# Two units moved in the queue of the second block's heads, and a weight sum made by a transfer that adds

## What is computed

```python
def _mla_block(qn, qr, qpos, kn, kr, v, kpos):
    logits = (jnp.einsum('bqhd,bkhd->bhqk', qn, kn, ...)
              + jnp.einsum('bqhr,bkr->bhqk', qr, kr, ...)) * MLA_SCALE
    mask = (kpos // CHUNK)[None, :] <= (qpos // CHUNK)[:, None]
    p = jax.nn.softmax(jnp.where(mask, logits, NEG_INF), axis=-1)
    return jnp.einsum('bhqk,bkhd->bqhd', p.astype(v.dtype), v)
...
    o = o.reshape(B, T, MLA_WIDTH) * jax.nn.silu(gate)
    return x + o @ w_out
```

## Time and profile before

| | us |
|---|---|
| median of 3 runs (2145.31 to 2145.38) | 2145.35 |
| the profiled execution: device time | 2145.84 |
| its span, first to last instruction | 2144.1 |
| TensorE busy | 2133.9 |
| VectorE busy | 1213.3 |
| ScalarE busy | 995.8 |
| GpSimd busy | 249.7 |

### The profile page before, as it was taken

How to read it: one execution, slowest core, us unless ns; L and a number is a source line. 1 busy time by engine, 2 the same in 40 slices (tenths; PEclk the granted TensorE clock), 3 DMA queues, 4 the chain that set the end, 5 groups by cost and what they waited for, 6 DMA issues and landing times.

```text
span 2144.1 us, 33654 instructions
## 1 busy us (share of the span) xinstructions
PE 2133.9 (100%) x11609; PEld 1870.8 (87%) x11609; DVE 1213.3 (57%) x2781; ACT 995.8 (46%) x2287; POOL 249.7 (12%) x261
## 2 busy tenths in 40 slices
PE   9999999999999999999999999999999999999999
PEld 7888888888888888888888988888899999998899
DVE  6555554545555555556223344443467777777986
ACT  5544444434444444453223433443366666665433
POOL 1000000000000000000000001421332001021011
PEclk9999999999999999999999999999999999999999
DMA  5333333333233333333442333343332212122451
GB/s 185 107 104 114 105 104 89 114 109 98 94 105 104 104 110 108 104 101 115 146 136 80 112 100 94 122 137 122 127 102 83 57 50 64 50 67 90 153 172 63
DMA packets 127462, 225.30 MB, mean 105 GB/s; under 512 B 21104, under 2 KB 75120, under 8 KB 127264
## 3 DMA queue, kind: packets, MB, share of 16 engines
q1 hardware_dynamic: 127392, 224.36, 33.4%
HBM read 191.42 MB, written 32.89 MB: 105 GB/s over the span
## 4 chain that ended last, share of the span: by engine, by line
PE 94%; DVE 3%; ACT 1%; issue 1%; DMA 1%; POOL 0%; SPq 0%; ACTq 0%; DVEq 0%; POOLq 0%
PE bank L214 67%; PE bank L2653 8%; PE bank L2004 4%; PE bank L961 1%; PE bank L937 1%; PE bank L2709 1%; PE bank L2687 1%; PE bank L2703 1%; PE bank L953 1%; PE bank L1997 1%; PE bank L2689 1%; PE bank L929 1%; PE bank L2681 1%; PE bank L271 0%; DVE h_tlo L1882 0%
## 5 line engine op out<-in xcount | busy, mean ns | idle before, releaser
L214 PE MATMUL bank<-b_whi,x_hi 128*128 128x512 f32 x1016 | 401.4, 395 | 0.2
L214 PE MATMUL bank<-b_whi,x_lo 128*128 128x512 f32 x1016 | 396.5, 390 | 0.0
L214 PE MATMUL bank<-b_wlo,x_hi 128*128 128x512 f32 x1016 | 396.5, 390 | 0.0
L197 DVE SCALAR_TENSOR_TENSOR b_wlo<-b_raw,first,b_whi 128x512 fp32r<-128x512 f32 x254 | 179.4, 747 | 140.8 <-ACT b_whi L184 139.8
L184 ACT ACTIVATE b_whi<-b_raw,first 128x512 fp32r<-128x512 f32 x254 | 169.4, 715 | 160.2 <-PE bank L214 133.1
L214 PEld LDWEIGHTS bank<-b_whi,x_lo 128*128 128x128 f32 x1016 | 190.7, 188 | 40.8
L214 PEld LDWEIGHTS bank<-b_whi,x_hi 128*128 128x128 f32 x1016 | 191.0, 188 | 36.6 <-DVE b_wlo L197 0.8
L214 PEld LDWEIGHTS bank<-b_wlo,x_hi 128*128 128x128 f32 x1016 | 191.0, 188 | 35.3
L214 PE MATMUL bank<-m_whi,x_hi 128*128 128x512 f32 x320 | 125.0, 391 | 0.0
L214 PE MATMUL bank<-m_wlo,x_hi 128*128 128x512 f32 x320 | 124.6, 389 | 0.0
L214 PE MATMUL bank<-m_whi,x_lo 128*128 128x512 f32 x320 | 124.6, 389 | 0.0
(11 more groups left out here) (547 smaller groups left out, 5362.9 us busy)
## 6 DMA issues: line engine op xcount, KB each, us to landing
b_raw<-w_fox SPq DMA_DIRECT2D x127, 512.0 KB, 3.5
m_raw<-w_mla SPq DMA_DIRECT2D x40, 512.0 KB, 3.5
c_raw<-w_out SPq DMA_DIRECT2D x32, 512.0 KB, 3.5
h_ring<-w_out2s SPq DMA_DIRECT2D x16, 768.0 KB, 6.0
f_raw<-w_ukv SPq DMA_DIRECT2D x16, 512.0 KB, 3.6
queries<-e_q SPq DMA_DIRECT2D x16, 480.0 KB, 4.5
e_raw<-w_uq SPq DMA_DIRECT2D x32, 192.0 KB, 2.5
f_qa<-queries SPq DMA_DIRECT2D x16, 320.0 KB, 3.7
```

The costliest lines, as they stand in the source:

```text
L197: op = eng.scalar_tensor_tensor(lo[:, k, :], raw[:, k, :], self.gain[:, K:K + 1], hi32[:, k, :], ALU.mult, ALU.subtract)
L214: op = eng.matmul(out, a, w[:, k, :], start=(first and k == 0 and i == 0), stop=(last and k == self.kk - 1 and i == len(pairs) - 1))
```

## The change

In `MlaHead.ORDER` T6 now stands between p2 and p1 (it stood behind p1), and T7 between p0 and g (it stood behind g). In `Fast` the signs are arranged so that each sum of weights is an addition into the first block; the sum that VectorE formed behind P6 (for P7) is now made by a transfer that GpSimd issues (`grow`), which loads a block from memory a second time and adds it to the one in the ring when P3's splits no longer need it. So VectorE forms three sums per round instead of four. The roles, ring slots and the sequence of loads follow from it; SP may issue the load of role 3 once the first sum is formed. Where a result has the other sign, an addition becomes a subtraction, and two of the four sums of activations use `scalar_tensor_tensor`.

```diff
-    ROLE = {"P1": 0, "P5": 0, "P6": 0, "P3": 2, "P7": 1, "P2": 2, "P4": 0}
-    FORMED = {"P5": 0, "P6": 1, "P7": 2, "P4": 3}
-    FORM_AFTER = {"P1": 0, "P5": 1, "P6": 2, "P2": 3}
+    ROLE = {"P1": 0, "P5": 0, "P6": 0, "P4": 0, "P3": 1, "P7": 1, "P2": 3}
+    LOADED = (0, 2, 1, 3)
+    FORMED = {"P5": 0, "P6": 1, "P4": 2}
+    FORM_AFTER = {"P1": (0, 2), "P5": (1, 1), "P2": (2, 3)}
+    SLOT = ((0, 1, 2, 2), (1, 0, 2, 2))
...
             for h in range(2):
-                self.formed.wait(sp, r, 8 + 2 * h + 2)
-                self.wait_split(sp, r, "P3", 2 * h + 1)
+                self.formed.wait(sp, r, 2 * h + 2)
                 self.load(sp, r, 3, h)
...
-                    self.formed.wait(sp, r, 12 + 2 * h + 2)
-                    self.wait_split(sp, r, "P2", 2 * h + 1)
-                    self.load(sp, r + 1, 1, h)
+                    self.formed.wait(sp, r, 8 + 2 * h + 2)
+                    self.load(sp, r + 1, 2, h)
...
-                    self.load(sp, r + 1, 2, h)
+                    self.load(sp, r + 1, 1, h)
...
-    def form(self, pool, r, j, u):
-        k = slice(2 * u, 2 * u + 2)
-        a, b, c = (self.ring[self.slot(r, i)][:, k, :] for i in range(3))
-        p, dst, x, y, role = (("P1", a, b, a, 1), ("P5", a, c, a, 2), (None, b, c, b, None), ("P6", a, c, a, 3))[j]
...
+    def grow(self, pool, r):
+        x = self.ring[self.slot(r, 1)]
+        for h in range(2):
+            self.wait_split(pool, r, "P3", 2 * h + 1)
+            pool.dma_start(x[:, 4 * h:4 * h + 4, :], self.w[r, 1, h], accum_op=ALU.add).then_inc(self.grown[h].sem, 16)
+
+    def form(self, dve, r, p, u):
+        i, role = self.FORM_AFTER[p]
+        k = slice(2 * u, 2 * u + 2)
+        x = self.ring[self.slot(r, 0)][:, k, :]
+        self.wait_split(dve, r, p, u)
+        self.arrived(dve, r, role, u)
+        dve.tensor_tensor(x, x, self.ring[self.slot(r, role)][:, k, :], ALU.add).then_inc(self.formed.sem, 1)
...
     def pool(self, pool):
         for r in range(self.ROUNDS):
+            self.grow(pool, r)
             self.join(pool, r, "P6")
             self.join(pool, r, "P7")
...
+        elif p == "P7":
+            self.grown[u // 2].wait(act_, r, 1)
...
     ORDER = ["kp", "T0", "T1", "s3", "ka", "T2", "s2", "new", "T3", "s1", "s0", "T8", "sa", "sb", "T4",
-             "p3", "T5", "pn", "p2", "p1", "T6", "on", "p0", "g", "T7", "ont", "qr", "qn", "o"]
+             "p3", "T5", "pn", "p2", "T6", "p1", "on", "p0", "T7", "g", "ont", "qr", "qn", "o"]
...
-        for role in range(3):
+        for role in (0, 2, 1):
             for half in range(2):
                 fast.load(sp, 0, role, half)
```

More of the change, by code:

```diff
@@ L1694, in __init__ @@
         self.in_ = [[s(f"h_in{i}{h}", 1, 16) for h in range(2)] for i in range(3)]
-        self.t_hi, self.t_lo, self.formed = s("h_t_hi", 4 * n), s("h_t_lo", 4 * n), s("h_formed", 16)
+        self.t_hi, self.t_lo = s("h_t_hi", 4 * n), s("h_t_lo", 4 * n)
+        self.grown, self.formed = [s(f"h_grown{h}", 1, 16) for h in range(2)], s("h_formed", 12)
         self.used, self.done = s("h_used", 3 * n), s("h_done", 2 * n)
@@ L1706, in slot @@
     def slot(self, r, role):
-        return (r + role) % 3
+        return self.SLOT[r][role]
     def view(self, x, k, q):
@@ L1727, in arrived @@
     def arrived(self, eng, r, role, u):
-        n = {0: 0, 1: 1, 2: 2, 3: 2}[role]
-        i = self.slot(r, n)
-        loads = [(q, role_) for q in range(self.ROUNDS) for role_ in range(4) if self.slot(q, min(role_, 2)) == i]
+        i = self.slot(r, role)
+        loads = [(q, x) for q in range(self.ROUNDS) for x in range(4) if self.slot(q, x) == i]
         self.in_[i][u // 2].wait(eng, 0, loads.index((r, role)) + 1)
     def load(self, sp, r, role, h):
-        i = self.slot(r, min(role, 2))
-        sp.dma_start(self.ring[i][:, 4 * h:4 * h + 4, :], self.w[r, role, h]).then_inc(self.in_[i][h].sem, 16)
+        i = self.slot(r, role)
+        sp.dma_start(self.ring[i][:, 4 * h:4 * h + 4, :], self.w[r, self.LOADED[role], h]).then_inc(self.in_[i][h].sem, 16)
     PIECES = [(0, 0), (1, 1), (0, 1), (1, 0)]
@@ L1827, in join @@
             x = self.R[:, 2 * a:2 * a + 2, n * self.N:(n + 1) * self.N]
-            pool.tensor_tensor(x, x, self.both[:], ALU.add).then_inc(self.joined.sem, 1)
+            pool.tensor_tensor(x, x, self.both[:], ALU.subtract if n else ALU.add).then_inc(self.joined.sem, 1)
     def pool(self, pool):
         for r in range(self.ROUNDS):
+            self.grow(pool, r)
             self.join(pool, r, "P6")
@@ L1838, in add_up @@
         a11, a12, a21, a22 = (self.view(self.o, k, q)[:, part, :] for q in range(2) for k in range(2))
-        dst, x, y, op = ((a22, a21, a22, ALU.add), (a21, a11, a21, ALU.subtract), (a11, a22, a11, ALU.subtract),
-                         (a12, a12, a11, ALU.subtract))[i]
+        n = (0 if part.start == 0 else 4) + i
         if i:
-            self.summed.wait(dve, 0, (0 if part.start == 0 else 4) + i)
-        dve.tensor_tensor(dst, x, y, op).then_inc(self.summed.sem, 1)
+            self.summed.wait(dve, 0, n)
+        if i < 2:
+            op = dve.tensor_tensor(*((a22, a22, a21, ALU.subtract) if i == 0 else (a21, a11, a21, ALU.subtract)))
+        else:
+            x, y = (a11, a22) if i == 2 else (a12, a11)
+            op = dve.scalar_tensor_tensor(x, y if i == 2 else x, -1.0, x if i == 2 else y, ALU.mult, ALU.subtract)
+        op.then_inc(self.summed.sem, 1)
     SPLIT_SUMS = ["P5", "P6", "P3", "P7"]
@@ L1874, in hi @@
             self.formed.wait(act_, r, 4 * self.FORMED[p] + u + 1)
+        elif p == "P7":
+            self.grown[u // 2].wait(act_, r, 1)
         elif u % 2 == 0:
-            self.arrived(act_, r, 3 if p == "P2" else self.ROLE[p], u)
+            self.arrived(act_, r, self.ROLE[p], u)
         self.before(act_, r, p, u)
@@ L1929, in take @@
                 y = self.both[:, m, :] if p == "P1" else self.bank(r, p, m)[:, 0:self.N]
-                dve.tensor_tensor(x, x, y, ALU.add).then_inc(self.taken.sem, 1)
+                dve.tensor_tensor(x, x, y, ALU.subtract if at and at[1] else ALU.add).then_inc(self.taken.sem, 1)
         if p in self.NEWS:
@@ L1939, in take @@
                 x = self.R[0:NEW, SM, n * self.N:(n + 1) * self.N]
-                dve.tensor_tensor(x, x, self.tmp[:], ALU.add).then_inc(self.new_added.sem, 1)
+                dve.tensor_tensor(x, x, self.tmp[:], ALU.subtract if p == "P1" and n else ALU.add).then_inc(self.new_added.sem, 1)
     def dve(self, dve, early):
@@ L1948, in dve @@
                     if p in self.FORM_AFTER:
-                        self.form(dve, r, self.FORM_AFTER[p], u)
+                        self.form(dve, r, p, u)
                     if r == 0 and u == 3 and j < len(self.SPLIT_SUMS):
```

## The result

The changed kernel takes 2153.85 us (median of 6 runs, 2152.85 to 2154.57) against 2145.40 for the kernel before: a ratio of 1.0037, 95% interval 1.0027 to 1.0047; the medians lie 8.4 us apart. The forecast was 2152.1. The profiled execution has a span of 2151.1 us.

A forecast was written before the change was run, and what follows sets the result against it. TensorE, busy 2133.9 of 2144.1 us, was taken as the bound, so only its waits could yield gains. From 2145.35, +9.5 in the heads and -2.8 in `Fast` gave 2152.1 us, range 2149.5 to 2158.0.

The forecast's parts named there:

- p1's wait covered, -0.23: Heads: T6 ahead of p1 covers p1's wait for VectorE's low half of p3, saving 0.23 us per head.
- g's copy behind g, +0.83 per head: Heads: without T7 behind g, qr waits for ScalarE's copy of g; 1.38 us against 0.55 of work.
- A head of 23.77: Steady loop: one head lengthens by 0.60 us from 23.17; the prediction's text gave 23.8.
- Body 15, +1.1: Body 15: `g_whi` in ScalarE's queue delays `f_on_lo`, p0's halves and the waiting qn by 1.1 us.
- `Fast`, -2.8: `Fast`, round one: fewer VectorE forms remove waits at P6's last unit (0.87) and P3's first (1.91); P6's first stays.
- The transfer hidden: `Fast`: GpSimd's adding transfers, 6.0 us plus some microseconds, land within slacks of 9.2 and 10.6 us, causing no wait.
- The estimate of 3.8 us: `Fast`: by the skill page, a GpSimd transfer takes 2.0 us plus bytes over 436 GB/s, here 3.8 us.
- `h_thi` of P7: Sign in `Fast`: ScalarE's `h_thi` splits for P7 would not wait for the adding transfer.
- Rival B: `Fast`: the adding transfer lands late and P7 waits; 2155.5 us at 12 us landing, 2162.7 at 15.6; chance 0.12.
- The sum: Whole kernel: +9.5 us in the heads and -2.8 in `Fast` on 2145.35, giving 2152.1 us.
- Rival C: Heads: qr does not feel g's copy, so no wait is left; 2138.7 us; chance 0.09.
- rival D: Heads: g to qr takes 0.97 us, not 1.38, so the edits level out at 2145.35 us; chance 0.05.

The follow-up runs named there:

- experiment 1: Kernel before with T6 moved ahead of p1 and T7 ahead of g in the heads, `Fast` untouched: 2156.49 us against 2145.93, ratio 1.0051.
- experiment 7: `Fast` change alone, old head order, round 0's last P5 form moved behind P6's first low half: 2142.95 us; with the softmax rates also moved on VectorE: 2149.12.
- Experiment 3: Kernel before with T6 alone moved ahead of p1, T7 in its old place behind g: 2150.34 us, ratio 1.0021.
- experiment 8: `Fast` change alone, old head order, each half's adding transfer made twice: 2160.42 us; with a writing transfer instead of the adding one: 2143.40.

## Why the prediction was right, and where its sizes were off

- **p1's wait covered, -0.23**: it is gone in the changed kernel and in experiment 1.
- **g's copy behind g, +0.83 per head from 1.38 us between g and qr**: measured 1.38. The reading that ScalarE is free when g ends held (0.59 us idle ahead of the copy). The parts differ a little: those of the forecast add up to 1.39, with 0.06 from the copy's end to the load and 0.10 from load to matmul, where the trace has 0.13 and 0.01. The wait was said to be 0.8 us at qr, 15 times. It is 0.62 at qr, 14 times, behind 0.25 at ont, where the forecast had 0.1 to 0.2; together 0.87. As forecast, ont's wait lies inside the stretch from g to qr and adds nothing to it.
- **A head of 23.77**: 23.82 on average. Up to body 14's qr the change costs 9.2 us and not the 8.4 of 14 x 0.60. The two terms themselves came out within 0.04, so where the rest lies stays open.
- **Body 15, +1.1**: +1.0, from one load of qr to the next (24.67 against 23.67). `f_on_lo` stood behind `g_whi` as forecast. The one that waits for it is ont (1.3 us), and not qn, which waits 0.2 as it did before. The size was right and the waiter was wrong.
- **`Fast`, -2.8**: -2.7 by the profiles, -2.6 by the timed runs. The two waits that were to go went, the third stayed, and P6's last low half starts where it was forecast (2025.2 on its scale). VectorE forms 24 sums in all, 12 a round.
- **The transfer hidden**: right, but by less than the prediction held. I took the plain loads' median of 6.0 and some microseconds; in the kernels with one adding transfer a half the first halves landed after 6.7 to 7.4, the second after 7.4 to 10.1, against slacks of 9.2 and 10.6. The estimate of 3.8 us that stands beside it was low for the writing transfer too (4.6). That two halves would be under way at once, and the later one the slower, was not in my working. One of the forecast's signs failed: `h_thi` of P7 does wait for the transfer, in both rounds, though TensorE doesn't. Rival B was near: without P6's wait, 0.86 us, the second half came late (experiment 7).
- **The sum**: +6.7 forecast, +7.5 in the profiles, +8.4 in the timed runs. Of the 1.7 us, 0.8 is in the loop's heads (the terms of body 15 and of `Fast` miss by 0.1 each, one either way). The rest is within the spread of the timed runs, and I can't assign it.
- **One reading that the forecast used was only half right.** The gain of T6's move was booked by itself; it lasts only while enough work stands between p1 and g. In the changed kernel T7 does. That the mark of -0.23 came out is due to both moves being made together; the forecast's own order of steps (T7 before g) had this in it, but did not say so, and it led me to expect -3.5 of T6 alone. Experiment 3 corrected that.

Rival C (no wait behind g) and rival D (0.97 us in place of 1.38) are excluded by the timeline of the head above.

## What to carry to other kernels

When TensorE is never idle for long, a unit of work in its queue probably covers something. Before you move one, write down both chains: the one that it is to cover (here 0.25 us) and the one that it covers now (for T6 the way from p1 through ScalarE and VectorE to g; for T7 the way from g through ScalarE's copy to qr, 1.38 us with 0.55 us of work in it). Move only as much work as the short wait asks for: three of T6's matmuls in place of twelve, and T7 left where it was, gave the gain in the loop's heads without a new wait. And when an engine's idle time in front of an instruction looks like a delay, ask what was computed in it: moving the rates behind it cost 6 us.

## What the runs showed of the hardware

- An adding transfer from GpSimd of 768 KB landed in 7.2 us at the median, a writing one in 4.6. Issuing one kept GpSimd for 0.9 to 1.1 us, a writing one for 0.5 to 0.8. With two under way the DMA engines were busy for 93 to 102% of the time and moved 188 GB/s adding and 309 writing, and the second adding one took up to 10.1 us.
- TensorE's granted clock stayed at 1.00 through waits of up to 1.9 us. In the wait of 7.5 us (it ended at 2048.6) it fell: a mean of 0.51 from 2045 to 2050, close to the lower of its levels, 1.2 GHz, 0.80 in the next 5 us, and 1.00 again from 2055. The wait of 5.9 us in round 1 (it ended at 2125.3) did the same: 1.00 to 2120, 0.86 in the next 5 us, 0.50 from 2125 to 2130. About 4 us of experiment 8's 17 are not in its two waits.
- The time up to the first head differs by over a microsecond between executions, though the program text ahead of it is the same. That is as much as some of the effects here; two marks inside the profile resolved what the totals could not.
